# Partition sums of the modulation rows: from one-row TensorE products to an all-reduce on GpSimd

## The chip, the core and the metric

The program runs on one core of a Trainium2 chip. A core has a matrix engine (TensorE, PE in the profile), a vector engine (VectorE, DVE), a scalar engine (ScalarE, ACT), GpSimd (POOL) and a sync engine (SyncE, SP) that issues transfers; ScalarE can issue transfers too (ACTq). Each engine runs its own instruction stream in order, and the streams meet at semaphores. The metric is the device time of one execution in microseconds (us).

## What is computed

Two transformer blocks of two layers each, batch 1, 256 tokens, width 1024, all in float32. What matters here is the modulation: a row per layer, made from a vector `c` that no token depends on, and added or multiplied to the activations in six places.

```python
c_act = jax.nn.silu(c)                      # 1 x 1024
for l in range(DEPTH):
    mod = c_act @ ada_w[l] + ada_b[l]       # ada_w[l]: 1024 x 6144
    sh_mix, sc_mix, g_mix, sh_ffn, sc_ffn, g_ffn = jnp.split(mod, 6, axis=-1)
    u = modulate(x, sh_mix, sc_mix)
    ...                                     # attention branches, gated and merged
    u = modulate(x, sh_ffn, sc_ffn)
    y = peer_ffn(u, ...)                    # experts: sum over e of w_e v_e gelu(u_e . x)
```

The second block computes its rows in the same way, `cs @ ada_w_2[i] + ada_b_2[i]`.

## The kernel before

The kernel is a sequence of stages (`stage`, L71), each closed by a barrier over all engines, after which GpSimd clears the semaphores of the stage. Two kinds of stage matter: the merge of the four attention branches (`merge_branches`, L1202, once per layer of the first block) and the dense evaluation of the experts (`experts`, L1755, likewise). Both are made of large float32 products that are computed as three products of split operands (`split_matmul`, L144: high by high, high by low, low by high). ScalarE writes the high part (L138) and VectorE the low part, the value less its high part (L141); so every weight tile that TensorE multiplies passes over both.

Beside this work the same stages compute the modulation rows of later layers in units of 512 columns. Per unit the 1024 x 512 weights arrive as eight slabs of 128 rows (four transfers of two), and VectorE does eight weighted additions of 128x512, each slab times a scalar per partition plus the accumulator (`scalar_tensor_tensor`, L360 in the expert loops, L1180 in the merges). That leaves `acc`, 128 partitions by 512 columns, whose sum over partitions is the row. There are 18 units in the expert stage of layer 0, 17 in that of layer 1, 6 and 3 in the two merges: 35 and 9.

**In the experts** (`SpreadModulation`, L311) the loop runs over 108 tiles of 128 experts in rounds of six (u = 0 to 5), one unit per round. On TensorE a tile is the hidden product of the next tile (`experts_ps_h`, 24 matmuls of 128x256), and then the tile's own product with the values (`expert_y`, 12 matmuls of 128x512). The weighted additions stand on VectorE at the end of tiles u = 0 to 3; at u = 4 TensorE multiplies `acc` by a column of ones between the hidden product and `expert_y` (`sum`, L363, a 1x512 result; the profile shows it as two matmuls); at u = 5 ScalarE copies the row out of PSUM and issues its store to DRAM (`keep`, L368), and at u = 0 of the next round it issues the load of the next bias and weights (`load`, L340). VectorE's order within a tile is: low part of the next tile's up weights in two halves (`u_lo`), the gate product (`experts_wgt`), low parts of the values and of the gates, and the weighted additions.

**In the merges** (`MergeModulation`, L1134) the loop runs over eight steps (half, branch) of three pieces, and TensorE does the one-row product after the first piece of the next step, into a bank of `ps_b`; before the third piece it waits until ScalarE has copied the row. SyncE issues the store.

The three tiles `mod_w`, `bias` and `acc` of the expert stage lie in the free part of `kept`, so they carry that name in the profile.

Of the kernel before, what the change touches and what calls it, by code (L numbers as in the profile page):

```python
# [10 lines left out]
ACT = mybir.ActivationFunctionType  # L11
ALU = mybir.AluOpType
AX = mybir.AxisListType

# [297 lines left out]
class SpreadModulation:  # L312
# [5 lines left out]
    def __init__(self, s, room, silu, ada_w, ada_b, mods, row):  # L318
# [4 lines left out]
        self.ones = s.sb("mod_ones", [P, 1])  # L323
        self.row = row
        self.ps = s.ps("mod_ps", [P, self.CW])
        self.w_in = [s.sem("mod_w_in0"), s.sem("mod_w_in1")]
        self.ready, self.added, self.summed = s.sem("mod_ready"), s.sem("mod_added"), s.sem("mod_summed")
        self.bias_in, self.row_done, self.stored = s.sem("mod_bias_in"), s.sem("mod_row_done"), s.sem("mod_stored")

    def begin_vector(self, dve):  # L330
        dve.memset(self.ones[:], 1.0)
        dve.memset(self.bias[:], 0.0).then_inc(self.ready, 1)
        dve.sem_inc(self.added, 1)
        dve.sem_inc(self.summed, 1)

    def begin_act(self, act):
        act.sem_inc(self.row_done, 1)
# [795 lines left out]
class MergeModulation:  # L1133
# [5 lines left out]
    def __init__(self, s, units, silu, ada_w, ada_b, row_out, first):  # L1139
# [5 lines left out]
        self.ones = s.sb("mod_ones", [P, 1])  # L1145
        self.row = s.sb("mod_row", [1, 2, self.CW])
# [3 lines left out]
        self.row_done = s.sem("mod_row_done")  # L1150
# [5 lines left out]
    def begin_vector(self, dve):  # L1156
        dve.memset(self.ones[:], 1.0)
# [2123 lines left out]
```

## Time and profile before

| | us |
|---|---|
| median of 3 runs | 3782.56 |
| lowest, highest | 3781.37, 3798.19 |
| the profiled execution | 3782.07 |
| its span, first to last instruction | 3780.3 |

The profile is one execution. Its page gives per engine the busy time, and the share of the span; a timeline row gives start, length, engine, line, operation and operand tiles, and in brackets how long the engine stood idle before it and what ended that. Lengths of matmuls overlap, so the price of one is read from the distance between starts. PEld is TensorE's weight load, and a "q" behind an engine's name is its instruction queue.

### The profile page before, as it was taken

To read this page: it belongs to the slowest core of one execution; us is meant where nothing else is said; L and a number is where in the kernel's file an instruction comes from. 1 tells how busy PE (TensorE), PEld (TensorE's weight loads), DVE (VectorE), ACT (ScalarE), POOL (GpSimd) and SP (SyncE) were. 2 spreads that over 40 slices of the span, in tenths; PEclk is the share of its full clock that TensorE was granted. 3 is DMA by queue.
4 is the path that set the end of the run, shared out by engine and by line. 5 is a ranking of instruction groups with operands and counts; after the bars stand their busy time and mean duration, and the time that the engine had idled before them with its cause. 6 is when DMAs were issued, how large, how long until landed. Compare 5 with 4: busy or idle time off the path is not lost. (4 is left out here: it accounts for less than half of the span.)

```text
span 3780.3 us, 60799 instructions
## 1 busy us (share of the span) xinstructions
PE 3431.6 (91%) x19918; PEld 2986.1 (79%) x19918; DVE 2550.6 (67%) x5089; ACT 1782.2 (47%) x3295; POOL 69.3 (2%) x62
## 2 busy tenths in 40 slices
PE   4989889899999987989799999999968799898798
PEld 3877777788888877878687788888857699687697
DVE  5478669777777765576589677777756466445565
ACT  2354327755555543444239555555533354444354
POOL 0010000000000000100000000000001100001000
PEclk8999999999999998999899999999989899999899
DMA  5327432277777755237231577777742143552253
GB/s 206 122 64 257 172 121 86 98 232 246 243 235 242 245 194 177 80 125 246 86 123 40 194 239 235 245 243 236 242 165 83 63 178 139 168 188 96 90 184 117
DMA packets 256318, 637.34 MB, mean 169 GB/s; under 512 B 39088, under 2 KB 66224, under 8 KB 250000
## 3 DMA queue, kind: packets, MB, share of 16 engines
q1 hardware_dynamic: 217924, 561.56, 44.5%
q10 hardware_dynamic: 38220, 73.55, 5.7%
q8 instruction: 98, 1.61, 0.2%
q14 instruction: 76, 0.62, 0.1%
HBM read 633.89 MB, written 1.15 MB: 168 GB/s over the span
## 5 line engine op out<-in xcount | busy, mean ns | idle before, releaser
L147 PE MATMUL experts_ps_h<-uP_lo,experts_u_hi 128*128 128x256 f32 x1728 | 488.9, 283 | 0.0
L148 PE MATMUL experts_ps_h<-uP_hi,experts_u_lo 128*128 128x256 f32 x1728 | 488.9, 283 | 0.0
L146 PE MATMUL experts_ps_h<-uP_hi,experts_u_hi 128*128 128x256 f32 x1728 | 487.8, 282 | 0.0
L138 ACT ACTIVATE experts_u_hi<-kept 128x512 fp32r<-128x512 f32 x432 | 269.1, 631 | 355.5 <-PE experts_ps_h L148 352.1
L141 DVE TENSOR_TENSOR experts_v_lo<-u_w,experts_v_hi 128x512 fp32r<-128x512 f32 x432 | 299.1, 692 | 164.8 <-ACT experts_v_hi L138 162.0
L141 DVE TENSOR_TENSOR experts_u_lo<-kept,experts_u_hi 128x512 fp32r<-128x512 f32 x432 | 291.8, 688 | 155.2 <-ACT experts_u_hi L138 142.1
L138 ACT ACTIVATE experts_v_hi<-u_w 128x512 fp32r<-128x512 f32 x432 | 272.2, 630 | 203.6 <-PE expert_y L148 203.2
L146 PE MATMUL expert_y<-experts_v_hi,experts_w_hi 128*128 128x512 f32 x864 | 343.1, 397 | 1.1 <-DVE experts_w_lo L141 1.1
L147 PE MATMUL expert_y<-experts_v_lo,experts_w_hi 128*128 128x512 f32 x864 | 338.3, 392 | 0.0
L147 PEld LDWEIGHTS experts_ps_h<-uP_lo,experts_u_hi 128*128 128x128 f32 x1728 | 330.9, 191 | 8.4
L146 PEld LDWEIGHTS experts_ps_h<-uP_hi,experts_u_hi 128*128 128x128 f32 x1728 | 330.8, 191 | 8.4
L148 PE MATMUL expert_y<-experts_v_hi,experts_w_lo 128*128 128x512 f32 x864 | 336.7, 390 | 0.0
L148 PEld LDWEIGHTS experts_ps_h<-uP_hi,experts_u_lo 128*128 128x128 f32 x1728 | 330.8, 191 | 0.0
L360 DVE SCALAR_TENSOR_TENSOR kept<-kept,silu 128x512 f32<-128x512 f32 x280 | 209.9, 749 | 11.9 <-DMA kept<-in_ada_w_all 6.0
L146 PEld LDWEIGHTS expert_y<-experts_v_hi,experts_w_hi 128*128 128x128 f32 x864 | 162.9, 188 | 60.0 <-issue 30.2
L146 PE MATMUL ffn_ps_u<-uP_hi,ffn_up_hi 128*128 128x256 f32 x704 | 200.0, 284 | 3.4 <-DVE ffn_up_lo L141 3.4
L147 PE MATMUL ffn_ps_u<-uP_lo,ffn_up_hi 128*128 128x256 f32 x704 | 199.5, 283 | 0.0
L148 PE MATMUL ffn_ps_u<-uP_hi,ffn_up_lo 128*128 128x256 f32 x704 | 199.4, 283 | 0.0
L148 PEld LDWEIGHTS expert_y<-experts_v_hi,experts_w_lo 128*128 128x128 f32 x864 | 162.3, 188 | 36.0
L147 PEld LDWEIGHTS expert_y<-experts_v_lo,experts_w_hi 128*128 128x128 f32 x864 | 163.0, 189 | 26.2
L138 ACT ACTIVATE merge_piece_hi<-turns 128x1024 fp32r<-128x1024 f32 x96 | 96.2, 1052 | 152.8 <-DMA turns<-in_w_gate 58.9
L1751 DVE TENSOR_SCALAR choose_col<-iota,slotT 128x128 f32<-128x128 f32 x512 | 163.7, 342 | 6.0 <-PE choose_ps_q L1588 5.3
(553 smaller groups left out, 8009.3 us busy)
## 6 DMA issues: line engine op xcount, KB each, us to landing
u_w<-in_peer_v SPq DMA_DIRECT2D x256, 512.0 KB, 4.3
kept<-in_peer_u SPq DMA_DIRECT2D x216, 512.0 KB, 4.3
kept<-in_ada_w_all ACTq DMA_DIRECT2D x140, 512.0 KB, 4.9
up_w<-in_ffn_w_up SPq DMA_DIRECT2D x44, 1024.0 KB, 5.5
od_in_w<-in_od_w_in SPq DMA_DIRECT2D x36, 1024.0 KB, 5.1
in_w<-in_w_in SPq DMA_DIRECT2D x48, 752.0 KB, 4.3
turns<-in_w_gate SPq DMA_DIRECT2D x32, 1024.0 KB, 6.1
down_w<-in_ffn_w_down SPq DMA_DIRECT2D x44, 512.0 KB, 3.4
```

What stands on the lines that cost most here:

```text
L138: return act.activation(self.hi[at], value, ACT.Copy)
L141: return dve.tensor_tensor(self.lo[at], value, self.hi[at].bitcast(F32), ALU.subtract)
L146: pe.matmul(out, left.hi[left_at], right.hi[right_at], start=start, stop=False, skip_group_check=skip)
L147: pe.matmul(out, left.hi[left_at], right.lo[right_at], start=False, stop=False, skip_group_check=skip)
L148: return pe.matmul(out, left.lo[left_at], right.hi[right_at], start=False, stop=stop, skip_group_check=skip)
L360: dve.scalar_tensor_tensor(out=self.acc[:], in0=self.w[:, q % 2, v], scalar=self.silu[:, m // 2, k:k + 1], in1=self.acc[:] if k else self. ...
L1751: ins = dve.tensor_scalar(col[:, n % 2, v], g.iota[:], slotT[:, 1, at], slotT[:, 2, at], ALU.is_equal, ALU.mult)
```

## The change

The product with ones, the copy out of PSUM and the semaphore `row_done` go, in both classes. In their place GpSimd gets a program in both stages: per unit it waits until the eight additions are done, and issues one `partition_all_reduce` over 128 partitions by 512 columns of float32, which reads `acc` in SBUF and writes the sum into all 128 partitions of `total`. The store takes partition 0 of `total` straight from SBUF. In the experts `total` is the first slab of the weights' tile `w`, so the first load of the next unit now also waits until the store has landed (`stored`), a wait that stands in ScalarE's stream. In the merges `total` is a double tile of its own.

```diff
 class SpreadModulation:
...
+        self.total = self.w[:, 0, 0]
...
     def load(self, sync, unit, m, col, q):
...
             sync.wait_ge(self.added, unit * KD + 1)
+            sync.wait_ge(self.stored, unit * 16 + 16)
             sync.dma_start(self.bias[0:1], self.ada_b[m].unsqueeze(0)[:, at]).then_inc(self.bias_in, 16)
...
-    def sum(self, pe, unit):
-        pe.wait_ge(self.added, unit * KD + (KD + 1))
-        pe.wait_ge(self.row_done, unit + 1)
-        pe.matmul(self.ps[0:1, :], self.ones[:], self.acc[:], start=True, stop=True).then_inc(self.summed, 1)
+    def sum(self, pool, unit):
+        pool.wait_ge(self.added, unit * KD + (KD + 1))
+        pool.sem_inc(self.begun, 1)
+        pool.partition_all_reduce(self.total, self.acc[:], P, REDUCE.add).then_inc(self.summed, 1)
 
     def keep(self, act, unit, m, col):
         act.wait_ge(self.summed, unit + 2)
-        act.wait_ge(self.stored, unit * 16 + 16)
-        act.activation(self.row, self.ps[0:1, :], ACT.Copy).then_inc(self.row_done, 1)
-        act.wait_ge(self.row_done, unit + 2)
-        act.dma_start(self.mods[m].unsqueeze(0)[:, bass.ds(col, self.CW)], self.row).then_inc(self.stored, 16)
+        act.dma_start(self.mods[m].unsqueeze(0)[:, bass.ds(col, self.CW)], self.total[0:1]).then_inc(self.stored, 16)
...
 class MergeModulation:
...
+        self.total = s.sb("mod_total", [P, 2, self.CW])
...
-    def sum(self, pe, n, bank):
-        pe.wait_ge(self.added, KD * (n + 1))
-        pe.matmul(bank[0:1, :], self.ones[:], self.acc[:, n % 2], start=True, stop=True).then_inc(self.summed, 1)
-
-    def keep(self, act, n, bank):
-        act.wait_ge(self.summed, n + 1)
+    def sum(self, pool, n):
+        pool.wait_ge(self.added, KD * (n + 1))
         if n >= 2:
-            act.wait_ge(self.stored[n % 2], 16 * (n // 2))
-        act.activation(self.row[:, n % 2], bank[0:1, :], ACT.Copy).then_inc(self.row_done, 1)
+            pool.wait_ge(self.stored[n % 2], 16 * (n // 2))
+        pool.sem_inc(self.begun, 1)
+        pool.partition_all_reduce(self.total[:, n % 2], self.acc[:, n % 2], P, REDUCE.add).then_inc(self.summed, 1)
...
 def merge_branches(nc, name, uP, oP, pre, merged, mod, then_load):
...
-                        if p == 2 and 1 <= n <= work.units:
-                            pe.wait_ge(work.row_done, n)
...
-                        if p == 0 and 1 <= n <= work.units:
-                            work.sum(pe, n - 1, bank_of(n - 1))
+
+            @block.gpsimd
+            def _(pool):
+                for n in range(work.units):
+                    work.sum(pool, n)
...
 def experts(nc, name, uP, table, kept, sources, pre_v, y, silu, ada, mods, spread):
...
+            @block.gpsimd
+            def _(pool):
+                def step(h, u, loads, unit, m, col):
+                    if m is not None and u == 4:
+                        work.sum(pool, unit)
+                work.begin_pool(pool)
+                rounds(pool, step)
```

How the instructions stand is shown in three places; line numbers of the changed kernel are its own. First TensorE in the expert loop at u = 4, before, where `experts_mod_ps` is the PSUM tile of the one-row result:

```order
L146 MATMUL experts_ps_h<-uP_hi,experts_u_hi 128x256
L147 MATMUL experts_ps_h<-uP_lo,experts_u_hi 128x256
L148 MATMUL experts_ps_h<-uP_hi,experts_u_lo 128x256
L364 ISA
L365 REGISTER_ALU
L366 MATMUL experts_mod_ps<-kept,experts_mod_ones 1x512
L1856 REGISTER_ALU
L1858 ISA
L146 MATMUL expert_y<-experts_v_hi,experts_w_hi 128x512
```

and the same place in the changed kernel:

```order
L147 MATMUL experts_ps_h<-uP_hi,experts_u_hi 128x256
L148 MATMUL experts_ps_h<-uP_lo,experts_u_hi 128x256
L149 MATMUL experts_ps_h<-uP_hi,experts_u_lo 128x256
L1844 REGISTER_ALU
L1846 ISA
L147 MATMUL expert_y<-experts_v_hi,experts_w_hi 128x512
L148 MATMUL expert_y<-experts_v_lo,experts_w_hi 128x512
L149 MATMUL expert_y<-experts_v_hi,experts_w_lo 128x512
```

The product and its waits are gone, and `expert_y` follows the hidden product directly. Second ScalarE at the end of u = 5 and over the branch to the next round, before (`slotT` holds the row, `kept<-in_ada_b_all` is the bias load):

```order
L138 ACTIVATE experts_v_hi<-u_w_1 128x512
L369 REGISTER_ALU
L370 ISA
L371 ACTIVATE slotT<-experts_mod_ps 1x512
L373 DMA modulations<-slotT 1x512
L1801 REGISTER_ALU
L1801 COMPARE_AND_BRANCH
L1801 UNCONDITIONAL_BRANCH
L345 ISA
L346 ISA
L346 DMA kept<-in_ada_b_all 1x512
```

and changed:

```order
L139 ACTIVATE experts_v_hi<-u_w_1 128x512
L370 REGISTER_ALU
L371 DMA modulations<-kept 1x512
L1789 REGISTER_ALU
L1789 COMPARE_AND_BRANCH
L1789 UNCONDITIONAL_BRANCH
L345 ISA
L346 ISA
L347 ISA
L347 DMA kept<-in_ada_b_all 1x512
```

The copy is gone, and a third wait (an ISA row, for the store to have landed) stands before the bias load. Third GpSimd from the end of the attention stage of layer 0 on, before, where the next work is the attention of layer 1:

```order
L827 UNCONDITIONAL_BRANCH
L76 ISA x141
L723 UNCONDITIONAL_BRANCH
L727 COPY turns<-proj 128x8x32 x2
L731 COPY turns<-turns 128x8x64 x2
```

and changed, where `merge_mod_total` and `kept` are the sums' outputs:

```order
L825 UNCONDITIONAL_BRANCH
L77 ISA x26
L1250 UNCONDITIONAL_BRANCH
L1184 ISA
L1184 ISA merge_mod_total<-merge_mod_acc 128x512 x6
L1212 UNCONDITIONAL_BRANCH
L77 ISA x76
L1864 UNCONDITIONAL_BRANCH
L1789 UNCONDITIONAL_BRANCH
L1789 ISA
L367 ISA kept<-kept 128x512
L1789 REGISTER_ALU
```

The six sums of the merge and the loop of the experts' sums have moved in between, with an ISA row ahead of the first sum of each loop.

## Rows read from the trace of the kernel before

**Rows 1.** The page: span; busy us, share of it and instructions of each engine.
```profile
span 3780.3 us, 60799 instructions
PE 3431.6 (91%) x19918; PEld 2986.1 (79%) x19918; DVE 2550.6 (67%) x5089; ACT 1782.2 (47%) x3295; POOL 69.3 (2%) x62
```

**Rows 2.** Busy by stretch: an expert stage, one merge step; then clock, DMA share, GB/s.
```profile
773.00:1402.00 629.00, 629.00 (x3930) 557.12 (x3928) 464.04 (x795) 340.03 (x665) 0.00 (x0) 1.00 0.73 238
347.36:364.85 17.49, 17.49 (x75) 13.53 (x74) 15.30 (x17) 7.41 (x8) 0.00 (x0) 1.00 0.84 300
```

**Rows 3.** Timeline of TensorE, one round of the first expert loop: start, length, line, operation.
```profile
1003.05 0.40 PE L146 MATMUL expert_y<-experts_v_hi,experts_w_hi 128*128 128x512 f32 x1
...
1008.67 0.40 PE L146 MATMUL expert_y<-experts_v_hi,experts_w_hi 128*128 128x512 f32 x1
...
1012.85 0.28 PE L146 MATMUL experts_ps_h<-uP_hi,experts_u_hi 128*128 128x256 f32 x1
...
1014.17 0.28 PE L148 MATMUL experts_ps_h<-uP_hi,experts_u_lo 128*128 128x256 f32 x1
1014.38 1.02 PE L366 MATMUL experts_mod_ps<-kept,experts_mod_ones 128*1 128x512 f32 x2
1015.33 0.50 PE L146 MATMUL expert_y<-experts_v_hi,experts_w_hi 128*128 128x512 f32 x1
...
1021.07 0.40 PE L146 MATMUL expert_y<-experts_v_hi,experts_w_hi 128*128 128x512 f32 x1
...
1023.82 0.28 PE L146 MATMUL experts_ps_h<-uP_hi,experts_u_hi 128*128 128x256 f32 x1
```

**Rows 4.** The product in the expert loops: count, ns min/median/max, first and last start.
```profile
L366 PE MATMUL experts_mod_ps<-kept,experts_mod_ones x70: 590/590/591, 805.1 to 2736.4; 128*1 128x512 f32 x70
```

**Rows 5.** Timeline of VectorE in the same round, and at the start of the next.
```profile
1008.72 1.51 DVE L141 TENSOR_TENSOR experts_u_lo<-kept,experts_u_hi 128x512 fp32r<-128x512 f32 x2
...
1022.15 1.29 DVE L141 TENSOR_TENSOR experts_u_lo<-kept,experts_u_hi 128x512 fp32r<-128x512 f32 x2 [2.39 <-ACT experts_u_hi L138]
```

**Rows 6.** Timeline of ScalarE at the end of that round; ACTq rows are DMA issues.
```profile
1018.93 0.57 ACT L371 ACTIVATE slotT<-experts_mod_ps 1x512 f32<-1x512 f32 x1
1019.54 0.28 ACTq L373 DMA_DIRECT2D modulations<-slotT  x1
1020.45 0.25 ACTq L346 DMA_DIRECT2D kept<-in_ada_b_all  x1
```

**Rows 7.** The product in the two merges: count, ns min/median/max, first and last start.
```profile
L1185 PE MATMUL merge_ps_b<-merge_mod_acc,merge_mod_ones x18: 591/592/592, 317.6 to 1728.7; 128*1 128x512 f32 x18
```

**Rows 8.** First merge, VectorE: one step; then the TensorE row that needs its first piece.
```profile
341.07 3.18 DVE L1180 SCALAR_TENSOR_TENSOR merge_mod_acc<-merge_mod_w,silu,merge_mod_acc 128x512 f32<-128x512 f32 x4
344.65 2.36 DVE L141 TENSOR_TENSOR merge_piece_lo<-turns,merge_piece_hi 128x1024 fp32r<-128x1024 f32 x2 [0.41 <-ACT merge_piece_hi L138]
...
347.36 0.39 PE L146 MATMUL merge_ps_g<-merge_piece_hi,uP_hi 128*128 128x512 f32 x1
```

**Rows 9.** Timelines of GpSimd and VectorE where both run: one overlap in attend, one in delta.
```profile
221.61 1.27 POOL L853 TENSOR_TENSOR attend_nat_bias<-attend_nat_bias,attend_nat_mask 128x512 f32<-128x512 f32 x1
...
216.44 0.48 DVE L1056 SCALAR_TENSOR_TENSOR branches<-attend_dtmp,attend_nlam 128x256 f32<-128x256 f32 x1
...
221.71 1.45 DVE L1056 SCALAR_TENSOR_TENSOR branches<-attend_dtmp,attend_nlam 128x256 f32<-128x256 f32 x1
...
2922.11 2.36 POOL L2424 TENSOR_TENSOR delta_C<-delta_L,delta_rows_mask 128x1024 f32<-128x1024 f32 x1
...
2923.64 0.85 DVE L2512 TENSOR_TENSOR delta_begc<-delta_egc,rates 128x8 f32<-128x8 f32 x1
```

**Rows 10.** GpSimd's two-input addition over 128x512: count | busy us, mean ns | idle before.
```profile
L853 POOL TENSOR_TENSOR attend_nat_bias<-attend_nat_bias,attend_nat_mask 128x512 f32<-128x512 f32 x16 | 21.1, 1320 | 1.3
```

**Rows 11.** DMA issues: KB each and median us from issue to landing.
```profile
out<-x SPq DMA_DIRECT2D x1, 1024.0 KB, 4.0
...
mix_norm_rows<-modulations SPq DMA_DIRECT2D x4, 8.0 KB, 1.6
```

More of the change, by code:

```diff
@@ L13 @@
 AX = mybir.AxisListType
+REDUCE = bass.bass_isa.ReduceOp
 P = 128
@@ L316, with __init__ @@
     CW = 512
-    def __init__(self, s, room, silu, ada_w, ada_b, mods, row):
+    def __init__(self, s, room, silu, ada_w, ada_b, mods):
         self.silu, self.ada_w, self.ada_b, self.mods = silu, ada_w, ada_b, mods
@@ L322, in __init__, with begin_pool @@
         self.acc = room.tile(self.CW)
-        self.ones = s.sb("mod_ones", [P, 1])
-        self.row = row
-        self.ps = s.ps("mod_ps", [P, self.CW])
+        self.total = self.w[:, 0, 0]
         self.w_in = [s.sem("mod_w_in0"), s.sem("mod_w_in1")]
         self.ready, self.added, self.summed = s.sem("mod_ready"), s.sem("mod_added"), s.sem("mod_summed")
-        self.bias_in, self.row_done, self.stored = s.sem("mod_bias_in"), s.sem("mod_row_done"), s.sem("mod_stored")
+        self.bias_in, self.stored = s.sem("mod_bias_in"), s.sem("mod_stored")
+        self.begun = s.sem("mod_begun")
     def begin_vector(self, dve):
-        dve.memset(self.ones[:], 1.0)
         dve.memset(self.bias[:], 0.0).then_inc(self.ready, 1)
         dve.sem_inc(self.added, 1)
-        dve.sem_inc(self.summed, 1)
+    def begin_pool(self, pool):
+        pool.sem_inc(self.summed, 1)
     def begin_act(self, act):
-        act.sem_inc(self.row_done, 1)
         act.sem_inc(self.stored, 16)
@@ L1149, in __init__ @@
         self.ready, self.added, self.summed = s.sem("mod_ready"), s.sem("mod_added"), s.sem("mod_summed")
-        self.row_done = s.sem("mod_row_done")
+        self.begun = s.sem("mod_begun")
         self.stored = [s.sem(f"mod_stored{v}") for v in range(2)]
@@ L1181, in add @@
                                      in1=acc if k else self.bias[:, n % 2], op0=ALU.mult, op1=ALU.add).then_inc(self.added, 1)
-    def sum(self, pe, n, bank):
-        pe.wait_ge(self.added, KD * (n + 1))
-        pe.matmul(bank[0:1, :], self.ones[:], self.acc[:, n % 2], start=True, stop=True).then_inc(self.summed, 1)
-    def keep(self, act, n, bank):
-        act.wait_ge(self.summed, n + 1)
+    def sum(self, pool, n):
+        pool.wait_ge(self.added, KD * (n + 1))
         if n >= 2:
-            act.wait_ge(self.stored[n % 2], 16 * (n // 2))
-        act.activation(self.row[:, n % 2], bank[0:1, :], ACT.Copy).then_inc(self.row_done, 1)
+            pool.wait_ge(self.stored[n % 2], 16 * (n // 2))
+        pool.sem_inc(self.begun, 1)
+        pool.partition_all_reduce(self.total[:, n % 2], self.acc[:, n % 2], P, REDUCE.add).then_inc(self.summed, 1)
     def store(self, sync, n):
-        sync.wait_ge(self.row_done, n + 1)
-        sync.dma_start(self.row_out.unsqueeze(0)[:, self.at(n)], self.row[:, n % 2]).then_inc(self.stored[n % 2], 16)
+        sync.wait_ge(self.summed, n + 1)
+        sync.dma_start(self.row_out.unsqueeze(0)[:, self.at(n)], self.total[0:1, n % 2]).then_inc(self.stored[n % 2], 16)
     def end_sync(self, sync):
@@ L1285, in _ @@
                             sigmoid(n - 1)
-                        if p == 2 and 1 <= n <= work.units:
-                            work.keep(act, n - 1, bank_of(n - 1))
                 sigmoid(STEPS - 1)
@@ L1752, in _, with experts @@
                     ins.then_inc(hot_done, 1)
-def experts(nc, name, uP, table, kept, sources, pre_v, y, slotT, silu, ada, mods, spread):
+def experts(nc, name, uP, table, kept, sources, pre_v, y, silu, ada, mods, spread):
     RING = 2
@@ L1786, in experts @@
         ps_h = s.ps("ps_h", [P, 2, 512])
-        work = SpreadModulation(s, Room(kept[:, IN_RING:].rearrange("p n t -> p (n t)")), silu, *ada, mods, slotT[0:1, 0:2].rearrange("p a t -> p (a t)"))
+        work = SpreadModulation(s, Room(kept[:, IN_RING:].rearrange("p n t -> p (n t)")), silu, *ada, mods)
         u_hi, u_split, u_used = s.sem("u_hi"), s.sem("u_split"), s.sem("u_used")
@@ L1872, in step @@
                         hidden(h + 1, u + 1)
-                    if m is not None and u == 4:
-                        work.sum(pe, unit)
                     add_up(h + EARLY, u, stop=is_last(h))
                 rounds(pe, step)
+            @block.gpsimd
[5 more added lines that the diff above has]
+                rounds(pool, step)
             @block.scalar
@@ L3087, in expert_layer @@
             y = stack.enter_context(nc.psum_tensor(f"expert_y{l}", [P, TB, D], F32))
-            experts(nc, f"experts{l}", uP, table, kept, up_weights, vs, y, slotT, g.silu, (a["ada_w_all"], a["ada_b_all"]), a["mods"], spread)
+            experts(nc, f"experts{l}", uP, table, kept, up_weights, vs, y, g.silu, (a["ada_w_all"], a["ada_b_all"]), a["mods"], spread)
         residual_norm(nc, f"ffn_out{l}", x, y, a["mods"][l][FFN_GATE:FFN_GATE + D], a["ln2_g"][l], a["ln2_b"][l])
```

5 lines of the change are left out of this document (removed).

## Prediction, made before the changed kernel ran

> **What bounds the kernel now.** I read the page first [rows 1]: TensorE is busy for 91% of the span, VectorE for 67%, GpSimd for 2%. That is an average, so I then took the busy times of the stages that the change touches [rows 2]. In the expert stage TensorE is busy for all of its 629.00 us at full granted clock, VectorE for 464.04 and GpSimd for none. In a merge step of 17.49 us TensorE is again busy throughout, but VectorE for 15.30. So in both places TensorE's stream is the clock, GpSimd is free, and VectorE follows, with room in the experts and hardly any in the merges. What matters further is that VectorE produces a part of every weight tile that TensorE multiplies: if it stops, TensorE stops as soon as what is split ahead is used up. Three further views decide: TensorE's timeline around the product [rows 3], VectorE's in the same round [rows 5], and the few places where GpSimd and VectorE now run at once [rows 9].
>
> **What is removed.** A tile of the expert loop takes 1008.67 - 1003.05 = 5.62 us on TensorE [rows 3]. The tile with the product should therefore have begun `expert_y` at 1008.67 + 5.62 = 1014.29, but did so at 1015.33, 1.04 us late, and the tile behind it took 1021.07 - 1015.33 = 5.74, another 0.12. So one unit costs 1.16 us, though its two matmuls show 590 ns each [rows 4]. There are 70 of them, so 35 units: 35 x 1.16 = 40.6 us. The merges have 18 such matmuls of the same length [rows 7], so 9 units, 9 x 1.16 = 10.4 us, if VectorE lets TensorE keep it. Together 51 us, all on the path. The copy out of PSUM (0.57 us per unit, row 1018.93) goes from ScalarE, which was not the bound, and is worth nothing by itself [rows 6].
>
> **What is added on GpSimd.** 44 all-reduces of 128x512. The trace has none, so its length D is bounded by the nearest row, an addition of two 128x512 operands on GpSimd, 1.27 us in one case [rows 9] and 1.32 as the mean of 16 [rows 10]. An all-reduce can't be shorter than one such pass: D is at least 1.3. For the upper end I count additions that follow one another if nothing overlaps and the sum over 128 partitions is made as eight groups of 16: 7 to fold the groups and 15 to fold 16 lanes one by one, 22 x 1.32 = 29 us. Between them: the lanes fold as a tree in 4 steps, 7 + 4 = 11 additions, 14.5 us without overlap; if the groups work side by side, 1 + 4 additions and a half-priced pass back, 7.3 us. I take the middle of these two, 10.9 us, because a hand-written routine that works on groups in parallel overlaps part of its steps and hardly all. That length would be free on GpSimd alone: the earliest consumer, ScalarE at the end of u = 5, comes at 1018.93 [rows 6], 10 us after the additions end near 1008.8 [rows 5].
>
> The GPSIMD Engine Reference of the Trainium skill (section Cross-partition, where GPSIMD wins) gives 247,699 ns for a reduction over partitions of 128x2048; a quarter of that is an estimate of 62 us for 128x512. No row here shows it.
>
> **What it stops.** GpSimd and VectorE meet in few places, and there one waits for the end of the other's instruction [rows 9]. At 221.61 GpSimd starts an addition that ends at 222.88. VectorE's row at 221.71, with two inputs in SBUF, takes 1.45 us where the same instruction took 0.48 at 216.44, and ends at 223.16, 0.28 after GpSimd. In delta an operation on 128x8, which has next to nothing to do, starts at 2923.64 and ends at 2924.49; GpSimd's instruction from 2922.11 on ends at 2924.47. So a GpSimd instruction that reads SBUF holds VectorE's two-input instructions off until it is over. Every low part (two inputs in SBUF) and every weighted addition is of that kind. The longest of these GpSimd rows is 2.36 us; whether an all-reduce, which is another kind of instruction, holds VectorE over its whole length is not shown, and I take it that it does, since both observed cases end with the GpSimd instruction to within 0.3 us.
>
> **How much of D is covered.** In the experts the additions of u = 3 end as the two halves of `u_lo` begin at 1008.72 [rows 5]. The first half goes ahead of GpSimd, to 1009.4; the second is held until 1009.4 + D and then takes 0.7. TensorE needs it at 1012.85, the start of its second six-k half [rows 3]. So 1012.85 - 1009.4 - 0.7 = 2.75 us are covered, and the rest stalls TensorE; what comes after (gate, value parts) follows in the same order and is not later than that. Per unit: D - 2.75 - 1.16 = D - 3.91. With 10.9 this is +6.99, and 35 x 6.99 = +245 us.
> In the merges VectorE's 15.30 us of a step and D no longer fit: 15.30 + D against 17.49 [rows 2] is D - 2.19 per unit. The stall of a single piece gives less: the additions end at 341.07 + 3.18 = 344.25, the next piece starts at 344.65 and its first half of 1.2 must be there at 347.36 [rows 8], so 1.9 are covered. VectorE as the bound is the later of the two: 9 x 8.71 = +78 us.
>
> **The wait for the store.** In the changed kernel the bias load at u = 0 waits for the store just issued. Without the copy the store starts near 1018.95, so the load can't start before 1018.95 + L, against 1020.45 before [rows 6]. `u_lo` then begins at 1022.15 and its first half is done at 1022.84 [rows 5]; TensorE needs it at 1023.82 [rows 3], 0.98 of cover. So it costs L - 1.5 - 0.98 per unit. The 8 KB load of rows lands in 1.6, the 1 MB store in 4.0 [rows 11]: between 0 and 1.5 us per unit, 0 to 53 us. I take 0, as 2 KB is nearest to the 8 KB row. The stores of the merges and the reload of GpSimd's routines lie in idle time of SyncE and GpSimd, and cost nothing as long as GpSimd has nothing else to do there, which is so in both stages [rows 2].
>
> **Sum.** 3780.3 + 245 + 78 = 4103.3 for the span, and 1.8 outside it (3782.07 less 3780.3) gives 4105 us. The profiled execution lies 0.5 us under the median, which is left aside.
>
> **Rivals.**
> *Hidden (faster).* The all-reduce does not hold VectorE, or is shorter than about 3 us. Then only the 51 us count: 3782.1 - 51 = 3731. For it: GpSimd is free, and D may reach 10 us unnoticed. Against it: both overlaps in [rows 9].
> *Hidden, but the store's wait eats it (no change).* As above with L = 4: 3731 + 53 = 3784. A D of 3.1 to 4.0 us with VectorE held ends in the same place, since 35 (D - 3.91) + 9 (D - 2.19) is zero at D = 3.56.
> *Held, at the upper end.* D = 29: 35 x 25.1 + 9 x 26.8 = 878 + 241 = +1119, 4901 us.
> *Held, at over 29 us.* A reduction whose lanes go through one routine column by column has no row here; every microsecond of D beyond 29 adds 44 us.
> With the estimate of 62 us from the GPSIMD Engine Reference of the Trainium skill this rival would give 35 x 58.1 + 9 x 59.8 = +2572, about 6354 us.
>
> **How the numbers follow.** Held with D between 4 and 29: 0.60, with its own range 3800 to 4901. Held and longer: 0.10. Hidden: 0.23. No change, by either way: 0.07. The single number is that of the likeliest case. The range has to take in the hidden case, since 0.33 would be left out otherwise: from 3728, a little under 3731 for the copy and the waits that go, to 4901. A difference of 0.5%, 19 us, is about what a measurement of this kernel can tell from none. Faster 0.23, same 0.07, slower 0.70.
>
> **What would show it.** In the changed trace: GpSimd rows of the sums give D directly. If VectorE is held, one `u_lo` or value row per round is as long as D, and TensorE shows one gap of D - 2.75 per round right after it, in which the granted clock may drop too; the round of the loop grows from 34.9 to about 41.9 us. If not, VectorE's 690 ns rows stay as they are, a round takes 33.7 us, and TensorE stays without a gap. The store's wait would show as a later `u_hi` on ScalarE at the start of a round. The forecast is wrong above all if D is far from 10.9 us, at 44 us per microsecond, or if an all-reduce does not hold VectorE as the additions do.

## The result, and the profile after

The changed kernel takes 3745.06 us (median of 4 executions, 3742.29 to 3748.66) where the kernel before takes 3788.13 on the same chip (3781.37 to 3798.19; a fourth execution, of 3793.7, has joined the three whose median stands ahead of the prediction as 3782.56). The ratio is 0.9891, with a 95% interval of 0.9863 to 0.9918: 1.1% faster, 43 us. Measured twice more beside later runs, it came to 0.9895 (0.9878 to 0.9911) and 0.9884 (0.9867 to 0.9902). The forecast was 4105 us, slower. Its range held the time; its direction was wrong.

The page of the kernel after, answering to [rows 1]: span, then busy time of each engine, then the low piece of the experts, and after it the two groups of all-reduces on GpSimd (count | busy us, mean ns | idle before).

```profile
span 3746.9 us, 60692 instructions
PE 3398.1 (91%) x19830; PEld 2989.5 (80%) x19830; DVE 2617.8 (70%) x5085; ACT 1756.9 (47%) x3251; POOL 224.5 (6%) x106
...
L142 DVE TENSOR_TENSOR experts_u_lo<-kept,experts_u_hi 128x512 fp32r<-128x512 f32 x432 | 354.2, 836 | 147.4 <-ACT experts_u_hi L139 135.6
...
L367 POOL PARTITION_ALL_REDUCE kept<-kept x35 | 122.2, 3492 | 1844.1 <-DVE kept L361 1844.1
L1184 POOL PARTITION_ALL_REDUCE merge_mod_total<-merge_mod_acc x9 | 33.0, 3663 | 255.4 <-issue 174.7 <-DVE merge_mod_acc L1176 80.7
```

An all-reduce of 128x512 lasts 3.49 us, not 10.9. GpSimd's share went from 2% to 6%, and VectorE's from 67% to 70% although nothing was given to VectorE. The low pieces of the experts show where the time went: their mean is 836 ns where it was 688 in the kernel before, and 432 x 148 ns are 64 us. VectorE is being held.

The timelines of one round in the kernel after: VectorE (the rows that answer to [rows 5]), then GpSimd, then TensorE's first value matmul of three tiles (to be read as [rows 3]), and the busy times of a round (from one all-reduce to the next).

```profile
828.95 3.33 DVE L142 TENSOR_TENSOR experts_u_lo<-kept,experts_u_hi 128x512 fp32r<-128x512 f32 x2
832.20 0.41 DVE L1947 TENSOR_TENSOR experts_wgt<-experts_hid,gate_table 128x256 f32<-128x256 f32 x1
```
```profile
829.24 3.49 POOL L367 PARTITION_ALL_REDUCE kept<-kept  x1 [30.23 <-DVE kept L361]
```
```profile
828.90 0.40 PE L147 MATMUL expert_y<-experts_v_hi,experts_w_hi 128*128 128x512 f32 x1
...
834.52 0.40 PE L147 MATMUL expert_y<-experts_v_hi,experts_w_hi 128*128 128x512 f32 x1
...
840.14 0.40 PE L147 MATMUL expert_y<-experts_v_hi,experts_w_hi 128*128 128x512 f32 x1
```
```profile
829.24:862.97 33.73, 33.73 (x218) 30.68 (x217) 27.20 (x45) 18.22 (x37) 3.48 (x1) 1.00 0.76 249
```

The two low pieces take 3.33 us instead of 1.51, so VectorE is held for 1.82 us. It is free again at 832.28, 0.45 us before GpSimd's row ends at 832.73. TensorE shows nothing of it: its tiles follow each other at 834.52 - 828.90 = 5.62 and 840.14 - 834.52 = 5.62 us, the length of a tile without a product in [rows 3]. The round is 33.73 us where it was 34.9, and TensorE is busy through all of it. The second half of the hidden product starts at 833.08, 0.80 us after the low pieces are done.

One merge step in the kernel after, VectorE, then GpSimd, then the busy times of the step (they answer to the merge step in [rows 2] and to [rows 8]):

```profile
345.52 4.40 DVE L142 TENSOR_TENSOR merge_piece_lo<-turns,merge_piece_hi 128x1024 fp32r<-128x1024 f32 x2
...
363.00 4.40 DVE L142 TENSOR_TENSOR merge_piece_lo<-turns,merge_piece_hi 128x1024 fp32r<-128x1024 f32 x2
```
```profile
345.84 4.00 POOL L1184 PARTITION_ALL_REDUCE merge_mod_total<-merge_mod_acc  x1 [14.80 <-DVE merge_mod_acc L1176]
```
```profile
345.52:363.00 17.48, 17.28 (x77) 13.99 (x76) 17.05 (x17) 6.94 (x7) 4.00 (x1) 1.00 0.94 324
```

The pair takes 4.40 us instead of 2.36, 2.04 more. The step lasts 363.00 - 345.52 = 17.48 us, as before [rows 2], but TensorE is no longer busy throughout (17.28) and VectorE nearly is (17.05). The bound has changed hands and the time has not moved.

**Where the 43 us come from.** Each stage is read from the first and last starts of its matmuls. An expert stage runs from the last matmul of the choice to the last of `expert_y`, a merge from the first of the gate to the last of the branch, in us:

| stage | before | after | after, second run | after, third run |
|---|---|---|---|---|
| first experts (18 units) | 695.1 | 674.0 | 675.9 | 676.6 |
| second experts (17 units) | 693.5 | 677.1 | 673.9 | 675.7 |
| first merge (6 units) | 141.4 | 137.6 | 137.5 | 136.3 |
| second merge (3 units) | 137.5 | 135.6 | 135.8 | 134.3 |

The experts give 37.5, 38.8 and 36.3 us in the three profiles, against 35 x 1.16 = 40.6. The merges seem to give 5.7, 5.6 and 8.3 against 10.4, but whole merge stages can't be compared. Up to the first matmul of the branch products (`merge_ps_b`), TensorE's mean granted clock is 0.80 to 0.90 of the upper level, another value in each execution whatever the kernel, and this part takes 14.1 to 15.7 us. Behind it the clock is 1.00 in every trace. Here is each merge in these two parts (us, first + rest):

| kernel | first merge | second merge |
|---|---|---|
| before | 14.6 + 126.8 | 14.5 + 123.0 |
| after | 15.7 + 121.9 | 15.7 + 119.9 |
| after, second run | 15.7 + 121.8 | 15.7 + 120.1 |
| after, third run | 14.6 + 121.7 | 14.4 + 119.9 |

Compared over the rest, at one clock, the merges give 8.0, 7.9 and 8.2 us. By whole stages the first profile gives 37.5 + 5.7 = 43.2, although the two spans of the first comparison differ by only 33.4. Most of the gap is in a stage that the change does not touch, the second attention. Here are its busy times before and after (TensorE first; the last three values are granted clock, DMA share, GB/s):

```profile
1569.30:1667.80 98.50, 81.12 (x618) 71.16 (x617) 71.67 (x194) 50.58 (x160) 16.14 (x16) 0.93 0.20 56
```
```profile
1544.80:1652.00 107.20, 90.34 (x617) 78.47 (x616) 72.17 (x193) 50.62 (x160) 16.07 (x16) 0.85 0.19 52
```

It took 8.7 us more with the same work, at a mean granted clock of 0.85 instead of 0.93 of the upper level. In a later profile of the same changed kernel that stage took 99.9 us at 0.93. So this belongs to the one execution and not to the change.

### The profile page after: what moved, and what is told of

Its sections match the earlier page's. It is cut to its first block and busy times, and to the rows that moved or that the text cites. A ratio compares the mean times of both kernels' runs of the same rounds, so it can differ in the third digit from the quotient of the medians.

```text
span 3746.9 us, 60692 instructions
## 1 busy us (share of the span) xinstructions
PE 3398.1 (91%) x19830; PEld 2989.5 (80%) x19830; DVE 2617.8 (70%) x5085; ACT 1756.9 (47%) x3251; POOL 224.5 (6%) x106
## 5 line engine op out<-in xcount | busy, mean ns | idle before, releaser
L142 DVE TENSOR_TENSOR experts_u_lo<-kept,experts_u_hi 128x512 fp32r<-128x512 f32 x432 | 354.2, 836 | 147.4 <-ACT experts_u_hi L139 135.6
L367 POOL PARTITION_ALL_REDUCE kept<-kept x35 | 122.2, 3492 | 1844.1 <-DVE kept L361 1844.1
```

The lines of the kernel that those rows point to most:

```text
L142: return dve.tensor_tensor(self.lo[at], value, self.hi[at].bitcast(F32), ALU.subtract)
L367: pool.partition_all_reduce(self.total, self.acc[:], P, REDUCE.add).then_inc(self.summed, 1)
```

## Experiments

**1. Each half of the change alone.** In `merge_pe` the class and the loop of the merges are those of the kernel before, and the experts are changed; in `experts_pe` it is the other way round. The line on which it turns, in the merges of `merge_pe` against the changed kernel:

```
-        pool.partition_all_reduce(self.total[:, n % 2], self.acc[:, n % 2], P, REDUCE.add).then_inc(self.summed, 1)
+        pe.matmul(bank[0:1, :], self.ones[:], self.acc[:, n % 2], start=True, stop=True).then_inc(self.summed, 1)
```

> The expert loops keep the all-reduces of the changed kernel, the two merges have the one-row TensorE products of the kernel before back. Theory (an all-reduce holds VectorE for about 2 of its 3.5 us; TensorE's stream covers that in the experts, where TensorE is the bound, and VectorE's own 15.3 us of a 17.5 us step leave no room for it in the merges): the gain is that of the experts alone, 35 x 1.16 = 41 us below the kernel before, and the changed kernel is no better than this one; a merge step is 17.5 us long. Rival (the merges give their 10 us and the loss is elsewhere): this one is 10 us slower than the changed kernel, about 31 us below the kernel before.

Measured: 3755.89 us, 0.9919 (0.9903 to 0.9935) of the kernel before (3784.62), so 28.7 us faster. By the medians that is nearer to the rival's 31 than to the theory's 41. Its stages are 675.8 and 676.5 us for the experts and 142.2 and 137.2 for the merges.

> The other half of the change: all-reduces in the merges alone, TensorE products in the experts. Theory: no difference from the kernel before to within 5 us, merge steps of 17.5 us, since the 1.16 us that leave TensorE come back as about 2 us during which VectorE is held. Rival (the hold is free in the merges too): 10 us faster, a step of 16.3 us.

Measured: 3779.65 us, 0.9982 (0.9972 to 0.9993), 5.0 us faster. Its experts take 695.8 and 694.0 us and its merges 136.5 and 134.2.

The theory said no difference within 5 us and the rival 10 us. By the stages it is neither: the merges give 7.9 us in their parts at full clock (122.0 and 119.9).

The halves add up to 33.7 us by the medians, and the whole gave 40 to 46 in three comparisons; why the medians fall short is not known. By stages they agree: each half moves its own stages and leaves the others as they were to within 1 us. Some 37 us of the gain are in the experts and some 8 in the merges.

**2. An all-reduce by itself, and what it holds.** A stage ahead of the first modulation runs streams of 40 small VectorE instructions on 128x128. Each stream has one all-reduce beside it, and afterwards the same streams run alone. Its core:

```
+                    for k in range(K):
+                        if k == 4:
+                            dve.sem_inc(go, 1)
...
+                    pool.wait_ge(go, i + 1)
+                    pool.partition_all_reduce(res[:, 0:N], src[:, 0:N], P, REDUCE.add).then_inc(summed, 1)
```

> The changed kernel with one more stage at its start that computes nothing of the output: GpSimd all-reduces of 128 to 1024 columns, alone and beside a stream of 40 small VectorE instructions (128x128) of three kinds: two inputs in SBUF, one in SBUF and one in PSUM, one in SBUF alone. Theory: alone the length D grows with the columns, near 0.3 us plus 6 ns per column (3.4 us at 512, 6.5 at 1024); the stream with two SBUF inputs grows by about 2 us at 512 columns, in proportion to the columns, so it is held during the reading and not during the whole of D; the streams with one SBUF input don't grow. Rival (held for all of D): the stream grows by D, 3.5 us at 512. Rival (the cost in the loops is a queueing effect and no hold): no stream grows by over 0.5 us.

Measured, GpSimd's timeline in that run. The rows from 19.66 on are 256, 512 and 1024 columns beside additions of two SBUF operands. Row 51.84 is 512 columns beside additions with one operand in PSUM, and row 59.81 beside a multiplication by a constant. The last two are 512 and 1024 columns with VectorE idle.

```profile
19.66 1.93 POOL L3059 PARTITION_ALL_REDUCE probe_res<-probe_src  x1 [0.99 <-DVEq L3037]
28.85 3.39 POOL L3059 PARTITION_ALL_REDUCE probe_res<-probe_src  x1 [7.26 <-DVEq L3037]
39.21 6.27 POOL L3059 PARTITION_ALL_REDUCE probe_res<-probe_src  x1 [6.96 <-DVEq L3037]
51.84 3.23 POOL L3059 PARTITION_ALL_REDUCE probe_res<-probe_src  x1 [6.37 <-DVEq L3037]
59.81 3.26 POOL L3059 PARTITION_ALL_REDUCE probe_res<-probe_src  x1 [4.73 <-DVEq L3037]
67.61 3.23 POOL L3059 PARTITION_ALL_REDUCE probe_res<-probe_src  x1 [4.53 <-DVEq L3033]
71.00 6.11 POOL L3059 PARTITION_ALL_REDUCE probe_res<-probe_src  x1 [0.17 <-DVEq L3033]
```

The VectorE instructions that were held are here, each the only one in its small window (duration in ns three times, then start):

```profile
L3040 DVE TENSOR_TENSOR probe_c<-probe_a,probe_b x1: 1182/1182/1182, 19.9 to 19.9; 128x128 f32<-128x128 f32 x1
```
```profile
L3040 DVE TENSOR_TENSOR probe_c<-probe_a,probe_b x1: 2332/2332/2332, 29.1 to 29.1; 128x128 f32<-128x128 f32 x1
```
```profile
L3040 DVE TENSOR_TENSOR probe_c<-probe_a,probe_b x1: 4625/4625/4625, 39.4 to 39.4; 128x128 f32<-128x128 f32 x1
```

An addition of this kind takes 0.28 us otherwise. The hold is therefore 0.90 us at 256 columns, 2.05 at 512 and 4.34 at 1024, in one piece. At 512 columns the held instruction begins about 0.3 us behind GpSimd's start (29.1 against 28.85) and ends about 0.8 us before GpSimd does (31.4 against 32.24). The all-reduce itself takes 3.2 us with nobody beside it. These are the theory's 3.4 and 6.5 us at 512 and 1024 columns to within 0.4. Its first case did not come out:

```profile
13.31 5.36 POOL L3059 PARTITION_ALL_REDUCE probe_res<-probe_src  x1 [12.87 <-issue]
```

This row, 128 columns and the first all-reduce of the kernel, takes 5.36 us, and its stream of 40 additions takes 8.20, as alone (it ends at 17.71, 4.4 us into the row). The first all-reduce of the next experiment takes 3.25 us for 512 columns, with nothing beside it. What fills the 5.36 is open.

> The changed kernel with a stage added ahead of the first modulation: streams of 40 VectorE instructions on 128x128, each kind once beside one all-reduce of 128x512 and once alone. It asks which kinds are held. Theory (what is held is an instruction that takes both of its operands from SBUF, or one operand at the faster rate; PSUM as a source frees it): streams of two SBUF operands (addition, multiply-add with an addition, and the addition written to PSUM) and the copy from SBUF grow by 2.0 to 2.1 us; the addition with one PSUM operand and the copy from PSUM by under 0.1. The sum over a row's elements from SBUF (one operand, no faster rate) is open: 0 or 2. Rival (whatever touches SBUF is held): all grow by 2, the streams from PSUM too, against the 8.04 us of the first probe's row. A first all-reduce with no stream beside it takes the cost of the first use out of the rows.

Measured, VectorE's timeline: the first seven rows are the streams with an all-reduce of 512 columns beside them, the last seven the same streams alone.

```profile
16.75 10.24 DVE L3041 TENSOR_TENSOR probe_c<-probe_a,probe_b 128x128 f32<-128x128 f32 x40 [7.30 <-POOL probe_res L3068]
27.10 12.60 DVE L3045 SCALAR_TENSOR_TENSOR probe_c<-probe_a,probe_b 128x128 f32<-128x128 f32 x40
39.80 8.26 DVE L3047 COPY probe_c<-probe_a 128x128 f32<-128x128 f32 x40
48.16 7.87 DVE L3049 TENSOR_REDUCE probe_c<-probe_a 128x1 f32<-128x128 f32 x40
56.12 8.04 DVE L3043 TENSOR_TENSOR probe_c<-probe_a,probe_ps 128x128 f32<-128x128 f32 x40
64.26 8.05 DVE L3051 COPY probe_c<-probe_ps 128x128 f32<-128x128 f32 x40
72.41 10.28 DVE L3053 TENSOR_TENSOR probe_ps<-probe_a,probe_b 128x128 f32<-128x128 f32 x40
82.79 8.20 DVE L3041 TENSOR_TENSOR probe_c<-probe_a,probe_b 128x128 f32<-128x128 f32 x40
91.09 10.59 DVE L3045 SCALAR_TENSOR_TENSOR probe_c<-probe_a,probe_b 128x128 f32<-128x128 f32 x40
101.77 5.62 DVE L3047 COPY probe_c<-probe_a 128x128 f32<-128x128 f32 x40
107.48 7.87 DVE L3049 TENSOR_REDUCE probe_c<-probe_a 128x1 f32<-128x128 f32 x40
115.44 8.05 DVE L3043 TENSOR_TENSOR probe_c<-probe_a,probe_ps 128x128 f32<-128x128 f32 x40
123.58 8.06 DVE L3051 COPY probe_c<-probe_ps 128x128 f32<-128x128 f32 x40
131.74 8.22 DVE L3053 TENSOR_TENSOR probe_ps<-probe_a,probe_b 128x128 f32<-128x128 f32 x40
```

Additions of two SBUF operands grow by 2.04 us, the multiply-add of the weighted additions by 2.01, the addition written to PSUM by 2.06, and the copy from SBUF by 2.64. The sum over a row, the addition with one operand in PSUM and the copy from PSUM do not grow at all. So the hold is real, but it depends on what the held instruction is and where it reads, and for two operands in SBUF it lasts about 2.05 of the all-reduce's 3.2 to 3.5 us. The Trainium skill (SBUF — State Buffer, Who interferes with whom) says that VectorE and GpSimd share one pair of ports as an exclusive lock, taken by VectorE's copies and by its two-input operations when both inputs are in SBUF, and not by instructions with at most one SBUF input outside the faster modes. All seven streams agree. For a GpSimd instruction against one of VectorE in a faster mode the same section says that whoever issues first has the pair for the whole instruction. Here the all-reduce's row outlasts the hold of the addition by 0.8 us, and the copy that was held longest lost 2.1 us to a row of 3.35. So it does not hold for its whole length, and the measurement decides.

**3. The experts: is the hold really covered?** `experts_nosum` leaves out the 35 all-reduces and stores the first partition of the accumulator:

```
-        pool.partition_all_reduce(self.total, self.acc[:], P, REDUCE.add).then_inc(self.summed, 1)
+        pool.sem_inc(self.summed, 1)
```

> The changed kernel without the 35 all-reduces of the experts; the first partition of the accumulator is stored as it is, so that part of the output is not the reference's. Theory (the hold of 2 us lies wholly inside the cover of 2.75 us): the same time as the changed kernel within 4 us, round 33.7 us, u_lo at 1.4 to 1.5 us for two. Rival (the hold leaks out now and then, by the 136 ns that the low pieces grew in the mean over 432 of them): up to 59 us under it.

Measured: 3737.05 us (3729.2 to 3742.85) beside 3736.73 for the changed kernel in the same minutes. The hold is gone from VectorE's timeline:

```profile
828.01 1.51 DVE L142 TENSOR_TENSOR experts_u_lo<-kept,experts_u_hi 128x512 fp32r<-128x512 f32 x2
```

The time is the same. The stages show a little more: 672.5 and 673.9 us for the experts in this trace against 676.6 and 675.7, 5.9 us less, and 3.4 to 5.9 less than in the three traces of the changed kernel. That is 0.1 to 0.2 us a unit, one trace against three, and the total does not show it. The gain of the experts is thus the removal of the products (with their copies on ScalarE, which no run took apart), and their all-reduces are all but free.

`experts_x2` and `experts_x4` run two and four all-reduces in series per unit (the diff is that of two; with four, the loop runs three times):

```
+        for t in range(1):
+            pool.partition_all_reduce(self.total, self.acc[:], P, REDUCE.add).then_inc(self.again, 1)
+            pool.wait_ge(self.again, unit * 1 + (t + 1))
+            pool.sem_inc(self.begun, 1)
         pool.partition_all_reduce(self.total, self.acc[:], P, REDUCE.add).then_inc(self.summed, 1)
```

> The changed kernel with two all-reduces in series for each of the 35 units of the experts in place of one. Theory (cover of 2.75 us in the round, each all-reduce holds about 2 us, the second one from 3.4 us behind the first's start): the first hold is covered, the second falls on the next low piece and comes to 4 us in all, 1.2 to 1.3 us past the cover: 35 x 1.2 = 42 us over the changed kernel, round 34.9 us. Rival 1 (the cover is larger than 4 us, or a hold costs no time to anybody): within 5 us of the changed kernel. Rival 2 (the hold is the whole of an all-reduce's 3.49 us, and the round has a larger cover than read): 7.0 - 3.5 = 3.5 us more of hold a unit, up to 120 us over it.

Measured: 3795.53 us, 53.7 over the changed kernel's 3741.8 beside it, 1.53 us per unit, and slower than the kernel before (1.0030, 1.0017 to 1.0042).

> The changed kernel with four all-reduces in series for each of the 35 units of the experts. Theory: 4 x 2.05 = 8.2 us of hold a unit, 8.2 - 2.75 = 5.45 past the cover, 35 x 5.45 = 190 us over the changed kernel, round 39.2 us; together with two all-reduces (5.45 and 1.3) the slope is 2.05 us for each further one. Rival 1 (nobody is delayed): the same time as with one. Rival 2 (whole length held): 14.0 - 2.75 = 11.2 us a unit, 390 us over it.

Measured: 3897.07 us, 155.3 over the changed kernel, 4.44 per unit. That one all-reduce is covered and a second is not came out, the slope did not: 1.53 for the second and (4.44 - 1.53) / 2 = 1.45 for each further one, not 2.05. VectorE's timeline with two shows why:

```profile
831.25 3.33 DVE L142 TENSOR_TENSOR experts_u_lo<-kept,experts_u_hi 128x512 fp32r<-128x512 f32 x2
...
835.44 2.46 DVE L142 TENSOR_TENSOR experts_w_lo<-experts_wgt,experts_w_hi 128x256 fp32r<-128x256 f32 x1
```

The first hold falls on `u_lo`, the second on `w_lo` (2.46 us instead of 0.41), which TensorE needs sooner. What TensorE waited for in 17 rounds of the first experts, with two and then with four (us in total, times, longest):

```profile
PE expert_y L147 <- DVE experts_w_lo L142: 18.6, 17, 1.6
PE experts_ps_h L147 <- DVE experts_u_lo L142: 2.8, 6, 0.7
```
```profile
PE expert_y L147 <- DVE experts_w_lo L142: 39.5, 33, 1.7
PE experts_ps_h L147 <- DVE experts_u_lo L142: 22.4, 16, 1.4
```

The holds do not pile up on one slack. Each falls on another piece with a cover of its own, and TensorE waits for `w_lo` by 1.1 us in the mean with two (18.6 / 17) and 1.2 with four (39.5 / 33), where the hold is 2.05. The waits make 21.4 / 17 = 1.26 us per unit with two and 61.9 / 17 = 3.6 with four. The remaining 0.3 and 0.8 stand in no row of waiting, and I leave them open.

**4. The merges: VectorE or the loads?** `merge_nosum` leaves out the nine all-reduces of the merges and stores the accumulator's first partition, as above; VectorE's first addition into an accumulator now waits for that store.

> The changed kernel without the nine all-reduces of the merges: partition 0 of the accumulator is stored in place of the sum, so these columns of the modulation are not the reference's. Theory (VectorE is the bound of a merge step once GpSimd holds it for 2 us): a step shrinks from 17.5 us to TensorE's own 16.3, some 10 us less in all than the changed kernel. Rival (the loads, at 300 GB/s and a DMA share of 0.84, are the bound): the step stays at 17.3 us or more and the time does not move.

Measured: 3741.17 us (3732.62 to 3759.64), 0.9896 of the kernel before, which does not separate it from the changed kernel; its trace does. Busy times of one step:

```profile
344.18:360.50 16.32, 16.32 (x74) 13.52 (x73) 15.10 (x16) 6.94 (x8) 0.00 (x0) 1.00 0.97 351
```

The step is 16.32 us, with TensorE busy throughout. 17.49 less 16.32 is 1.17, the price of one unit's product with its two matmul rows. The same loads now arrive in 16.32 us, so they never were the bound at 17.48. In their parts at full clock the merges take 119.4 and 119.5 us, which is 7.4 and 3.5 less than before: 9 units at 1.2. The changed kernel gave 8.0 of these 10.9, so the hold eats some 3 us. The theory's 10 us less than the changed kernel did not come: the step shrank as it said, but not every step had been that long.

`merge_timed` keeps the all-reduces and moves their start in time, so that the hold meets the one instruction of the step that reads PSUM:

```
-    def sum(self, pool, n):
+    def sum(self, pool, n, split):
         pool.wait_ge(self.added, KD * (n + 1))
+        pool.wait_ge(split, 2 * ((n + 1) * MergeWeights.PER + 1) + 1)
...
-                    if n <= work.units:
-                        work.store(sync, n - 1)
+                        if p == 1 and 2 <= n <= work.units + 1:
+                            work.store(sync, n - 2)
```

> The changed kernel; in the merges the all-reduce of a unit starts one instruction before VectorE's product with a PSUM operand (L1287) instead of right behind the unit's last addition, and the row's store is issued later by as much. Theory (GpSimd takes from VectorE about 2.05 us of a port of SBUF, from 0.3 us behind its own start; an instruction with one operand in PSUM runs through it, as 40 of them did in the added stage of the probe, 8.04 us with and without an all-reduce): the 1.2 us of L1287 lie in the held stretch, only about 0.7 us are left to delay the next instruction, the merge step is 15.3 + 0.7 = 16.0 us of VectorE's work, less than TensorE's 16.32, and it falls from 17.48 to 16.3 to 16.4; 9 units by 1.1 us: about 10 us under the changed kernel. Rival (any instruction of VectorE is delayed beside an all-reduce, wherever it reads; or the step of 17.48 is the loads' and not VectorE's): the step stays at 17.3 to 17.5 and the time within 2 us of the changed kernel's.

The changed kernel ran beside it:

> The changed kernel once more, as the measure for the runs beside it, on the chip and in the minutes of theirs. Both theories: 38 to 44 us under the kernel before (3745 against 3788 in its first measurement).

Measured: 3737.56 us, and 3741.8 for the changed kernel. VectorE's and GpSimd's rows, and the busy times of the step:

```profile
347.85 1.21 DVE L1288 TENSOR_TENSOR merge_part<-merge_sig,merge_ps_b 128x1024 f32<-128x1024 f32 x1
349.21 1.90 DVE L1291 TENSOR_TENSOR merged<-merged,merge_part 128x1024 f32<-128x1024 f32 x1
```
```profile
346.99 4.04 POOL L1185 PARTITION_ALL_REDUCE merge_mod_total<-merge_mod_acc  x1 [12.07 <-DVE merge_piece_lo L142]
```
```profile
347.85:363.95 16.10, 16.10 (x72) 13.33 (x71) 15.67 (x17) 6.94 (x7) 4.03 (x2) 1.00 1.00 361
```

The product with the PSUM operand runs through at 1.21 us, and the addition behind it takes 1.90 instead of 1.23: a hold of 0.67, where 0.7 was expected. The step falls from 17.48 to 16.10 on VectorE's timeline (TensorE's own work is 16.32, so VectorE makes up a little there), and TensorE is busy throughout again. At full clock the merges take 119.5 and 119.5 us, as if there were no all-reduce. But that is 2.3 and 0.6 us less than the changed kernel beside it (121.8 and 120.1), some 3 us and not 10. I had counted all nine units, while in the changed kernel's first merge only two steps show the full 17.48. In the step behind them the first branch of the second half of the columns is added up: its product goes straight to its place, VectorE has one addition of 1.2 us less to do, and the step is 16.3 us long. The second merge has one step of 17.48 in the run beside this one, and none in the other two.

> The kernel with the timed all-reduce in the merges a second time, against the changed kernel in the same minutes. By the first run's traces its merges are 3.5 and 1.8 us shorter (134.0 and 134.0 against 137.5 and 135.8), so 5.3 us are expected; the rival is that they are lost behind, and it takes the same time within 2 us.

> The changed kernel a third time, for the runs beside it: 38 to 44 us under the kernel before.

Measured: 3734.27 us (3730.78 to 3748.84), and 3736.73 for the changed kernel, 46 us under the kernel before. Over both pairs the medians are 3736.2 us (8 executions) and 3737.57 (9). The size of 1 to 4 us is within the spread of either kernel, and so a gain in the total is not shown.

The 5.3 us that were expected of the merges did not come back either. Whole, they take 135.1 and 135.1 us against 136.3 and 134.3, which is 0.4 us less. The first merge in its two parts, in the changed kernel and then with the timed all-reduce (the third value from the end is the granted clock):

```profile
291.40:306.00 14.60, 14.60 (x65) 12.67 (x66) 12.34 (x14) 5.92 (x6) 0.00 (x0) 0.87 0.86 309
306.00:427.70 121.70, 120.89 (x528) 98.44 (x527) 102.82 (x96) 51.09 (x51) 22.48 (x6) 1.00 0.80 283
```
```profile
297.40:313.00 15.60, 15.60 (x64) 13.41 (x65) 12.30 (x14) 5.91 (x6) 0.00 (x0) 0.80 0.88 314
313.00:432.50 119.50, 119.50 (x529) 98.92 (x528) 98.27 (x96) 51.02 (x51) 23.47 (x6) 1.00 0.83 285
```

This time the timed kernel had the lower clock at the start, in the first pair the changed one had (0.80 against 0.87). At full clock the parts are 119.5 and 119.5 against 121.7 and 119.9: 2.6 us less, after 2.9 in the first pair. So a gain of some 3 us in the merges is shown twice, and the other half of the 5.3 was the clock of those executions.

## Why the prediction was wrong

**The removal: right.** 1.16 us for each of the 35 units was taken from [rows 3]. The experts gave 37.5, 38.8 and 36.3 us in three profiles against 40.6, and 42.2 without their all-reduces.

**The length of an all-reduce: wrong, and the largest error.** The step put D at 10.9 us, midway between 7.3 and 14.5, and built on a count of additions of the kind in [rows 10]. It is 3.49 us, 2.6 times the row of an addition. The measured value lies near the low bound of 1.3, and no row of the trace spoke for the number of passes that the estimate assumed. At 44 us per microsecond this term alone was worth 7.41 x 44 = 326 us of the 360 that the forecast missed by. The estimate of 62 us from the GPSIMD Engine Reference of the Trainium skill, which stood beside it, is for another operation and lay further off still.

**"Held for the whole of D": wrong.** With the measured D the prediction's own formula gives 35 x (3.49 - 3.91) + 9 x (3.49 - 2.19) = -14.7 + 11.7 = -3 us, no change. That a hold exists was right, and so was its place in the second half of `u_lo`. The two overlaps of [rows 9] were ordinary GpSimd additions, and they did not carry over. The all-reduce holds for about 2.05 us (1.82 in the round shown), and the rest of its row stops nobody.

**The cover of 2.75 us: borne out, but the formula let it go below zero.** "D - 2.75 - 1.16" treats an unused cover as a gain: with a hold of 2 us it would give more than the removal. It should read: the excess over the cover, or zero, less 1.16. With 1.8 us under a cover of 2.75 the excess is zero. In the round shown 1.82 us of hold left 0.80 of slack, so 2.62 were covered. A second all-reduce in series took all of the gain back, but its hold fell on `w_lo`, a piece that the prediction had counted as covered along with `u_lo`, so that run does not measure this cover.

**The merges: right mechanism, wrong size.** VectorE does become the bound: busy 17.05 of 17.48 us. The step of the prediction with H for the hold, 15.30 + H against 17.49, gives -0.14 at H = 2.05, and the steps came to 17.48. It was applied nine times, but only two or three steps were that full, and the merges gained 8 us at full clock.

**The store's wait: no cost seen.** At the end of a round in the kernel after, the bias load is issued at 840.36, 2.76 us behind the store at 837.60. With L = 2.76 the prediction's formula gives 0.28 us per unit, 10 us; TensorE has no gap there. The zero came from L taken near 1.6, and that was short of the 2.76 seen.

**Put together**, the stages measured 36 to 39 us for the experts and 8 for the merges, 44 to 47 us, against -43, -40 and -46 in the three comparisons. The rival called "hidden" gave 3731, nearest to the measured 3745, but neither of its conditions was met as written: the all-reduce does hold VectorE, and at 3.49 us it is not shorter than about 3. Its second clause is true only if the hold is meant. By its length alone, D stood in the rival that forecast no change (3.1 to 4.0 us). The range held the time because it reached from the hidden case to the longest one, not because the likeliest case was right.

## What to carry to other kernels

Before an unknown instruction is priced by a chain of assumed passes, take the low bound and the high bound as two cases and ask which answer each gives; here the change of sign lay at 3.56 us, near the low one. An all-reduce's interference with VectorE is not "busy at the same time": it is a hold that covers part of its length, and of the kinds tried it met only instructions that read two operands from SBUF, and copies and multiplications from SBUF at the faster rate. So count its length against the slack of the very piece it falls on, and never count unused slack as a gain. Where VectorE has no slack, start the all-reduce so that its hold meets an instruction that reads PSUM; here that gave some 3 us in the merges and nothing that the total shows. And before two stages are compared by their length, compare their granted clocks.

## What the runs showed of the hardware

- An all-reduce over 128 partitions takes 1.93, 3.39 and 6.27 us for 256, 512 and 1024 columns beside two-operand additions, and 3.23 and 6.11 us for the last two with VectorE idle.
- It holds a VectorE addition of two SBUF operands for 0.90, 2.05 and 4.34 us of these, in one piece. The first all-reduce of one kernel (128 columns, 5.36 us) held none of the additions that ran beside its first 4.4 us; why is open. Beside the long pieces of the merges its row is 4.00 us instead of 3.49, which would fit a wait for VectorE's running instruction; that was not tested.
- A copy from SBUF to SBUF is held for longer, 2.64 us, and a multiplication by a constant likewise: 8.31 us for 40 beside an all-reduce against 5.61 alone. Both run at the faster rate otherwise (5.6 against 8.2 us for 40). The longest single instruction was held for 2.1 us and some behind it were slower too; why was not looked into.
- Sums along a row, the addition with an operand in PSUM and the copy from PSUM ran through it at their own pace.
- The first 14.1 to 15.7 us of a merge ran at a mean granted clock of 0.80 to 0.90, different between executions of one kernel; the rest of it at 1.00.
